# Hybrid Hyena/GLA layer with a PEER expert mixer on one Trainium2 core: two of five token tiles by gathered rows instead of one, their values summed on TensorE in 32-column groups

## What is computed

```python
def peer_ffn(h, wq, sub_keys, u_tab, v_tab):
    q = (x @ wq).reshape(T, PEER_HEADS, 2, PEER_DQ // 2)      # 8 heads, two halves of 128
    s = jnp.einsum('thpd,hpkd->thpk', q, sub_keys)            # 128 sub-keys each
    s_top, i_top = lax.top_k(s, 16)
    cand_s = s_top[:, :, 0, :, None] + s_top[:, :, 1, None, :]
    cand_i = i_top[:, :, 0, :, None] * 128 + i_top[:, :, 1, None, :]
    best, pos = lax.top_k(cand_s, 16)
    idx, gate = take_along_axis(cand_i, pos), softmax(best)
    a = gelu(einsum('td,tkd->tk', x, u_tab[idx]))             # 128 experts per token
    y = einsum('tk,tkd->td', gate * a, v_tab[idx])
```

## Time and profile before

| | us |
|---|---|
| median of 3 runs | 2315.78 (2309.94 to 2328.16) |
| profiled execution | 2312.32 |
| span of its trace | 2310.5 |
| PE busy in the span | 2174.2 (94%) |
| DVE / POOL / ACT busy | 1439.6 / 797.5 / 624.0 |
| data moved by DMA | 475.54 MB |

### The profile page before, as it was taken

The page is one execution under the profiler, slowest core; times in us unless marked ns, Lnnn a source line. Parts: engine busy times, 40 slices in busy tenths (PEclk is TensorE's granted clock), DMA queues, the critical chain, the costliest instruction groups (busy, mean ns, idle before and its releaser), DMA issues.

```text
span 2310.5 us, 30679 instructions
## 1 busy us (share of the span) xinstructions
PE 2174.2 (94%) x9868; PEld 1663.6 (72%) x9868; DVE 1439.6 (62%) x3055; ACT 624.0 (27%) x930; POOL 797.5 (35%) x713
## 2 busy tenths in 40 slices
PE   6999989598998899999989999999999999999998
PEld 2554444445997787787868777787888888888886
DVE  4222322623889999788868877324766666666665
ACT  2111022233212222333323323223322323223232
POOL 0000001002323555799979999101221222212210
PEclk8999998798999999999999999999999999999999
DMA  9122134105102444599988999755988888888883
GB/s 339 41 73 73 42 109 153 64 35 191 62 13 96 155 141 136 165 292 296 301 268 288 302 284 301 233 202 184 359 287 289 292 285 294 287 287 294 285 292 145
DMA packets 293477, 475.54 MB, mean 206 GB/s; under 512 B 148871, under 2 KB 150055, under 8 KB 292872
## 3 DMA queue, kind: packets, MB, share of 16 engines
q1 hardware_dynamic: 256520, 340.20, 44.6%
q0 software_dynamic: 36864, 134.23, 16.4%
HBM read 401.76 MB, written 72.61 MB: 205 GB/s over the span
## 4 chain that ended last, share of the span: by engine, by line
PE 64%; POOL 9%; DVE 5%; issue 2%; DMA 2%; ACT 1%; SPq 1%; DVEq 0%; ACTq 0%; POOLq 0%
PE ps L959 30%; PE ps L900 19%; POOL eB L1846 6%; PE ps L837 3%; POOL ugat L1815 3%; PE ps L872 2%; PE ps L873 2%; PE ps L940 2%; PE ps L719 1%; SPq L523 1%; DMA ugat<-in_u_rows,idx 1%; DMA uraw<-in_u_t 1%; PE ps L861 1%; PE ps L819 0%; DVE h2T L1293 0%
## 5 line engine op out<-in xcount | busy, mean ns | idle before, releaser
L900 PE MATMUL ps<-h2hi,uhi 128*128 128x512 f32 x1024 | 449.1, 439 | 23.4 <-POOL ulo L1803 8.3
L900 PE MATMUL ps<-h2hi,ulo 128*128 128x512 f32 x1024 | 405.5, 396 | 0.0
L959 PE MATMUL ps<-vhi,whi 128*128 128x512 f32 x1024 | 399.8, 390 | 5.2 <-DVE wlo L1467 5.2
L900 PE MATMUL ps<-h2lo,uhi 128*128 128x512 f32 x1024 | 403.6, 394 | 0.0
L959 PE MATMUL ps<-vlo,whi 128*128 128x512 f32 x1024 | 399.7, 390 | 0.0
L959 PE MATMUL ps<-vhi,wlo 128*128 128x512 f32 x1024 | 399.5, 390 | 0.0
L1823 POOL DMA_INDIRECT vgat<-in_v_tab,idx x128 | 149.8, 1170 | 654.7 <-DVE y L1477 504.8
L1846 POOL TENSOR_SCALAR eB<-iota,jcur 128x128 f32<-128x128 f32 x384 | 315.9, 836 | 15.9 <-DVE jcur L1432 14.0
L1465 DVE TENSOR_TENSOR vlo<-vraw,vhi 128x1024 fp32r<-128x1024 f32 x128 | 156.8, 1225 | 216.3 <-ACT vhi L1739 216.3
L1739 ACT ACTIVATE vhi<-vraw 128x1024 fp32r<-128x1024 f32 x128 | 135.5, 1061 | 464.4 <-PE ps L959 462.0
L940 PEld LDWEIGHTS ps<-eA,eB 128*128 128x128 f32 x1024 | 189.8, 189 | 90.0 <-POOL eB L1846 29.9
(11 more groups left out here) (270 smaller groups left out, 2908.7 us busy)
## 6 DMA issues: line engine op xcount, KB each, us to landing
uraw<-in_u_t SPq DMA_DIRECT2D x128, 512.0 KB
vraw<-in_v_tab SPq DMA_DIRECT2D x128, 512.0 KB
gelu_scratch<-aout SPq DMA_DIRECT2D x128, 256.0 KB
gate_scratch<-gst SPq DMA_DIRECT2D x16, 2048.0 KB
ain<-gelu_scratch SPq DMA_DIRECT2D x128, 256.0 KB, 4.2
gin<-gate_scratch SPq DMA_DIRECT2D x128, 256.0 KB, 4.4
wring<-in_w_ada SPq DMA_DIRECT2D x12, 2048.0 KB, 7.8
wring<-in_w_in SPq DMA_DIRECT2D x6, 2048.0 KB, 8.4
```

Of the source, the lines that this page charges most:

```text
L900: last = pe.matmul(ps[:, b % 4, :], w[:, b % 2, k, :], h[:, k, LP:T], start=(k == 0 and j == 0), stop=(k == KD - 1 and j == 2))
L959: last = pe.matmul(ps[:, y_bank(t) + h, :], w[:, b, (t - 1) * P:t * P], v[:, b, h * 512:(h + 1) * 512], start=(start and j == 0), stop=(st ...
```

## The change

- NSP = 2: tiles 0 and 1 go the gathered way (256 tokens); TD becomes 384, three dense tiles. First products have 384 columns, second products are 18 per block. The query products are cut in 256 and 384 columns instead of 320 and 320.
- BLK_A is 48; stage B has 48 blocks (three tiles of 16); stage C has 32 (96 to 127).
- 256 u gathers and dots: 96 in stage B (2 a block, as before), 96 in stage C (3 a block), 64 in the blocks 0 to 31 of the second pass (2 a block).
- The values of the two tiles are no longer added on DVE. For each token POOL gathers its 128 v rows onto the 128 partitions (index column from `idxT`, the turned index; eight buffers `vgat`). The 128 weights of a token are put in one column of a 128 x 32 matrix of zeros (`wcol`), and PE multiplies it with the gathered rows: four tokens to a step, one in each group of 32 output columns, 2 x 4 products of 512 columns (plain float32). 64 such steps stand behind every second block: from block 111 of stage C to block 45 of the second pass for tile 0, from block 50 to block 112 for tile 1.
- gate_scratch is [half tile, partition, block, 64 tokens]: a store is one run of 16 KB per partition; the gates are loaded for four blocks in one DMA in runs of 1 KB.
- The GELU tile is 192 KB a block. h2hi, h2lo and many buffers are placed elsewhere; POOL starts h2lo only when the last output projection is done; the prompt's and the second tile's h2 rows are turned on PE (four more transposes for two halves), and the second tile's rows wait in `h2turn` for a copy after the last query product.
- The loops over registers become unrolled code in several places.

```diff
-TD = T - P
+CG = 32
+NSP = 2
+LSP = NSP * P
+TD = T - LSP
 NTD = TD // P
-BLK_A = 40
+BLK_A = 48
+VSLOT = 8
+DOTS_T = 3
+DOTS_V = 2
+GELU_0 = BLK_C + -(-(HK - NTD * DOTS_IT) // DOTS_T)
+TURN_0 = GELU_0 + 2
+STEP_0 = range(TURN_0 + 2 - NBLK, TURN_0 + 2 - NBLK + 2 * CG, 2)
+GELU_1 = (NDOT - DOTS_A) // DOTS_V
+TURN_1 = STEP_0[-1] + 3
+STEP_1 = range(TURN_1 + 2, TURN_1 + 2 + 2 * CG, 2)
...
-    g_dram = nc.dram_tensor("gate_scratch", [NBLK, P, TD], F32, kind="Internal").ap()
+    g_dram = nc.dram_tensor("gate_scratch", [NHALF, P, NBLK, THALF], F32, kind="Internal").ap()
...
-                sp_.dma_start(g_dram.rearrange("i p (c t) -> c p i t", t=64)[bass.ds(c, 1)]
-                              .rearrange("o p i t -> (o p) i t")[:, ii], gst[:, half, ii]).then_inc(g_stored[half], 16)
+                sp_.dma_start(g_dram[bass.ds(c, 1)].rearrange("o p i t -> (o p) i t")[:, ii], gst[:, half, ii]
+                              ).then_inc(g_stored[half], 16)
...
+            def load_gates(m):
+                if m >= 2:
+                    sp_.wait_ge(w_ready, R2 * (m - 1))
+                sp_.dma_start(gin[m % 2][:].rearrange("p c i t -> p c (i t)"),
+                              g_dram[:, :, R2 * m:R2 * (m + 1), :].rearrange("c p i t -> p c (i t)")).then_inc(g_landed[m % 2], 16)
...
-                        last = pe.matmul(ps[:, b % 4, :], w[:, b % 2, k, :], h[:, k, LP:T],
+                        last = pe.matmul(ps[:, b % 4, 0:TD], w[:, b % 2, k, :], h[:, k, :],
...
+            def weights_to_slots(t):
+                pe.wait_ge(w0_ready, t + 1)
+                pe.transpose(ps[:, 4, 0:P], dots[:, t, :], ident[:]).then_inc(w_turned, 1)
+
+            def value_step(t, r):
+                if r == 0:
+                    pe.wait_ge(wcol_ready, t + 1)
+                g = (t * CG + r) * NCG
+                for c in range(NCG):
+                    pe.wait_ge(v_gathered[(g + c) % VSLOT], 16 * ((g + c) // VSLOT + 1))
+                for h in range(2):
+                    for c in range(NCG):
+                        last = pe.matmul(ps[c * CG:(c + 1) * CG, 4 + h, :], wcol[t][:, c, r, :],
+                                         vgat[(g + c) % VSLOT][:, h * 512:(h + 1) * 512], start=(r == 0), stop=(r == CG - 1))
+                last.then_inc(v_used, 1)
...
+            for n in range(NBLK - R2):
+                second_ready(n)
+                for t in range(NSP, NT):
+                    last = second_products(n % R2, t, n == 0, False)
+                last.then_inc(s2_used, 1)
+                for t, r in steps_at(n):
+                    value_step(t, r)
...
+            dve.wait_ge(h2row_ready, 1)
+            for t in range(NSP):
+                best_experts(t)
+                seq(dve.scalar_tensor_tensor(selw[:, t, 0], selw[:, t, 0], float(NKEYS), selw[:, t, 1], ALU.mult, ALU.add))
+                dve.tensor_copy(idxs[:, t], selw[:, t, 0]).then_inc(idx_ready, 1)
...
+            for n in range(BLK_C, NBLK):
+                if n + 1 < NBLK:
+                    split_u(n + 1, n + 1)
+                for g in tail_dots(n):
+                    dot(g)
...
+            for n in range(NBLK):
+                if n + 1 < NBLK:
+                    weight(n + 1)
+                low_parts(n)
+                for g in value_dots(n):
+                    dot(g)
...
-                    add_value(it, b, first)
...
+            def gather_v(g):
+                if g >= VSLOT:
+                    pool.wait_ge(v_used, (g - VSLOT) // NCG + 1)
+                t, r, c = g // P, (g % P) // NCG, g % NCG
+                tok = c * CG + r
+                pool.indirect_dma_start(out=vgat[g % VSLOT][:], out_offset=None, in_=v_tab,
+                                        in_offset=bass.IndirectOffsetOnAxis(ap=idxT[:, t, tok:tok + 1], axis=0)
+                                        ).then_inc(v_gathered[g % VSLOT], 16)
...
+            for n in range(BLK_C, NBLK):
+                for g in tail_dots(n):
+                    gather_u(g + GSLOT)
+                if n == BLK_C + 2:
+                    for b in range(2):
+                        pool.wait_ge(g_stored[b], 32 * NTD)
+                    pool.memset(wcol[0][:], 0.0).then_inc(wcol_zero, 1)
+                if n == TURN_0 - 1:
+                    for g in range(VSLOT):
+                        gather_v(g)
+                for t, r in steps_at(n - 1 - NBLK):
+                    for c in range(NCG):
+                        gather_v((t * CG + r) * NCG + c + VSLOT)
+            for n in range(NBLK):
+                for g in value_dots(n):
+                    gather_u(g + GSLOT)
+                if n == 1:
+                    pool.wait_ge(h_full, NBLK)
+                    pool.memset(wcol[1][:], 0.0).then_inc(wcol_zero, 1)
+                for t, r in steps_at(n - 1):
+                    for c in range(NCG):
+                        gather_v((t * CG + r) * NCG + c + VSLOT)
```

More of the change, by code:

```diff
@@ L85 @@
 KD_1 = 2
-CG = 32
 KV_ORDER = [(0, "f"), (0, "b"), (1, "f"), (4, "b"), (2, "f"), (3, "b"), (3, "f"), (2, "b")]
@@ L427, in bass_hybrid_layer @@
         a_landed = [sem(f"a_landed{b}") for b in range(4)]
-        g_landed = [sem(f"g_landed{b}") for b in range(4)]
+        g_landed = [sem(f"g_landed{b}") for b in range(2)]
         vhi_ready = sem("vhi_ready")
@@ L848, in _ @@
                 ada_cols(i)
-            for h in range(2):
-                transposes(f"hr{h}", [h2T[:, 4 * h + j, 0:P] for j in range(4)])
+            for t in range(NSP):
+                for h in range(2):
+                    transposes(f"hr{t}{h}", [h2T[:, 4 * h + j, rows(t)] for j in range(4)])
             pe.wait_ge(ld_keys, 16)
@@ L918, in slots_to_rows @@
                 for j in range(3):
-                    last = pe.transpose(ps[:, 6 + d % 2, j * P:(j + 1) * P], selw[:, 1 + d, j, :], ident[:])
+                    last = pe.transpose(ps[:, 6 + d % 2, j * P:(j + 1) * P], selw[:, NSP + d, j, :], ident[:])
                 last.then_inc(cl_full, 1)
+                if d == NTD - 1:
+                    for t in range(NSP):
+                        last = pe.transpose(ps[:, 5, rows(t)], selw[:, t, 0, :], ident[:])
+                    last.then_inc(idx_turned, 1)
             loop(pe, BLK_A // 4 - 1, step_a)
@@ L1381, in _ @@
                     best_keys(t, h)
-            for t in range(1, NT):
+            for t in range(NSP, NT):
                 best_experts(t)
@@ L1480, in step_2 @@
-            def step_2(it, first, last):
-                for b in range(TOPK):
-                    n = it * TOPK + b
-                    if not (last and b == TOPK - 1):
-                        weight(n + 1, (b + 1) % R2, it * 64 + 16 * ((b + 1) // R2 + 1))
-                    low_parts(n, b % R2)
-                    add_value(it, b, first)
-            slot_weights(NTD - 1)
-            weight(0, 0, 16)
-            step_2(0, True, False)
-            with dve.Fori(1, IT_2 - 1) as it:
-                step_2(it, False, False)
@@ L1700, in stage, with slot_gelu @@
                                    ACT.Copy).then_inc(gate_staged, 1)
-            def slot_gelu(r, first):
-                act.wait_ge(dot_done, DOTS_IT * (r + 1))
-                if not first:
-                    act.wait_ge(w0_ready, r)
-                act.activation(acur[:], dots[:], ACT.Gelu_apprx_tanh).then_inc(dots_gelu, 1)
+            def slot_gelu(t):
+                act.wait_ge(dot_done, HK * (t + 1))
+                act.activation(dots[:, t], dots[:, t], ACT.Gelu_apprx_tanh).then_inc(dots_gelu, 1)
             for b in range(4):
@@ L1718, in _, with step_b @@
                 pair(n, n % 4, False, False)
-            def step_b(it, first, second):
+            def step_b(it, first):
                 for b in range(NB_B):
@@ L1831, in _ @@
             pool.wait_ge(idx_ready, 1)
-            for k in range(GSLOT):
-                gather_u(k)
+            for g in range(GSLOT):
+                gather_u(g)
             with pool.Fori(POOL_FROM // 4, BLK_A // 4) as it:
```

428 lines of the change are left out of this document (223 added, 205 removed).

## The result

The changed kernel takes 2361.86 us (median of 4 runs, 2357.52 to 2376.02); the kernel before took 2314.65 us beside it (4 runs, 2309.94 to 2328.16). The ratio is 1.0207, with a 95% interval of 1.0156 to 1.0258. The forecast was 2288 us: the time lies inside the range, but the direction is wrong, 2% slower where 1.2% faster was forecast. The interval shows a slower kernel; whether by more or less than 2% it leaves open.

A forecast was written before the change was run, and what follows sets the result against it. It took PE to bound the second pass, DVE's search stage A, and POOL beside PE stage B. Terms: 707 + 239 + 358 + 247 + 720 + 9 + 3 = 2283 us of span, 2288 as median; range 2230 to 2375.

The forecast's parts named there:

- Front: Ahead of stage A: added turns, moves and a later h2lo cost some 2 us (bounds 0 and 5), 707 us.
- A: Stage A: DVE's top-16 search still ends it, so PE's gain is nearly lost; 239 us.
- So I take 7.34: Stage B: POOL's round is 7.34 us a block once 256-byte gate stores go; 48 x 7.34 + 6 = 358 us.
- POOL stays at 8.26: Stage B rival: slow rounds come from DVE and gathers, not gate stores; 44 us more, 2332; chance 0.07.
- At 390: Behind stage B: transfers run at 390 GB/s, giving stage C 247 us and the second pass 720 us.
- slow rival: Block 108 to second-pass block 112: engines give 354 GB/s, u gathers queue behind v gathers; 2359 us; chance 0.25.
- their 81: Stage C, blocks 96 to 107: 12 x 6.0 us plus 9 for first loads of the second pass, 81 us.
- Blocks 0 to 32: Second pass, first 33 blocks: transfers bound them, 100.1 MB at 390 GB/s, 257 us.
- Blocks 33 to 112: Second pass: PE is full, 80 x 4.09 + 39 x 1.85 = 399 us, three lost, 402 us.
- the rival of 6.89: Value steps: the four column groups run one after the other, 6.89 us a step; 2482 us; chance 0.03.
- the 1.85 us of `ada`: Value steps on PE: 1.85 us each, read from eight like products, with the tiling-mode change taken as inside.
- the three that were to be lost: Second pass, blocks 33 to 112: 3 us lost beyond PE's 399, making 402.

The follow-up runs named there:

- experiment 6: Kernel before and changed kernel each run once more, unchanged: 2321.03 us and 2370.51 us (one run each).
- e4: Kernel before with the partition-major gate scratch alone: 2312.43 us (10 runs), ratio to before 0.9993.
- e7: Changed kernel with stage B's dots replaced by one-element copies (96 of 256 dots missing): 2295.7 us (one run).
- e8: Kernel before with both the partition-major gate scratch and four of eight eB rows on DVE: 2288.99 us (4 runs), ratio to before 0.9850.
- e6: Kernel before with four instead of two of eight eB rows on DVE: 2345.84 us (4 runs), ratio to before 1.0092.
- e5: e3 with two of the four value gathers of a step issued one block later: 2300.55 us (4 runs), ratio to before 0.9922.
- e1: Changed kernel with six u buffers instead of four and six v buffers instead of eight: 2384.0 us, ratio to before 1.0264.
- e12: e5 with the u gathers behind stage B cut to half of each row: 2243.17 us (one run).
- e3: Changed kernel with four instead of two of eight eB rows on DVE: 2313.91 us (10 runs), ratio to before 0.9983.
- e9: e5 with the u gathers behind stage B cut to 64 of 128 partitions: 2331.62 us (one run).

## Why the prediction was wrong

- **Front, +13.** As much can come with an execution alone (experiment 6). The means of the five profiles with the old front and the nine with the new are 714 and 721 us; how much of these 7 us is the change's, for which the prediction had 2, stays open.
- **A, +2.** Right for its stated reason: DVE's search ended it. The 2 us are the reading's: the prediction began B before at 942, where its first product stands at 947, and from 241.3 us A went to 241.7. The search itself was held up more. DVE's L1445 took 4158 ns on average, 3327 in the same operation before: each record takes 2.29 or some 4.37 us, every slow one with POOL's ulo beside it for more than 2 us, and 9 of 10 are slow instead of 4.
- **B, +29: a step that failed.** It said that POOL's slow rounds come with the gate stores, "So I take 7.34". e4 gave 514 us with the stores mended, as before, and rows no faster (858 ns on average, 836 before). What sets the round is DVE: a row takes 1.40 us beside a long DVE operation and 0.62 without (e7). The rival "POOL stays at 8.26" had the right mechanism and 0.07 of the chances; 8.06 was measured. So the shorter round never came: on average it was 8.03 us before (514 / 64) and 8.06 after. The gate layout isn't worthless, but its worth appears only once the rows have been moved (e8 against e6: 59 us in B).
- **C, +38: the larger step that failed.** "At 390" took one rate for all that stands behind B. In C the transfers gave 355 GB/s, because they were not asked for in time: the u gathers queue behind batches of four value gathers. The slow rival named this order, but priced it as a lower rate of the engines. Reordering gives 18 us in C (e5), two more u buffers 27 (e1). The rate is 26 of the 38 us: C moved 101 MB (285 us at 355 GB/s), and at 390 they take 259. Of these 26, 23 are in blocks 108 to 127 (66 MB at 344 GB/s). The other 12 are bytes: 95.9 MB were counted, and forgotten were the last two gate stores, 4 MB, which are issued at the start of C. They are most of what blocks 96 to 107 took over their 81.
- **Blocks 0 to 32, -14.** Right mechanism (bytes, e12), rate too low: 415 instead of 390. The Trainium skill (DMA: Bandwidth & Descriptors, Specifications) puts the limit of HBM at about 358 GB/s per core. It is no ceiling here: 415 held for 243 us. So the total near the slow rival's 2359 is luck: that rival wanted 354 GB/s up to block 112 and nothing lost in B, and the time came from B and C.
- **Blocks 33 to 112, +7.** PE full, as forecast. Column groups in parallel, as forecast; the rival of 6.89 falls. A small step of the prediction fails here: it read the price of changing between the two kinds of products as inside the 1.85 us of `ada`. It stands outside, and a step cost 2.10 us: 39 x 0.25 = 10 us, less the three that were to be lost and weren't.

B and C together are 67 of the 74 us, enough to turn 1.2% faster into 2% slower. In words: PE lost 151 us of busy time, but the whole kernel moves 101 MB more (576.66 against 475.54), and of the four stretches behind A only the last is PE's. With stage B cured and the gathers in the other order (e5) the change is worth 0.8%; the same cure of stage B in the kernel before (e8) is worth 1.5% without it. So in the forms measured here the second gathered tile gains nothing over a kernel of four dense tiles whose stage B runs well: behind the front both take the same, 1574 us in e5 and 1576 in e8, and the medians are 2300.55 and 2288.99.

## What to carry to other kernels

Before work moves from a full engine to the transfers, sum the bytes for each stage and ask when each gather can be issued, behind which others on its queue: a rate that the engines can give isn't reached by an order that asks late. Take the duration of a small GpSimd operation by what VectorE does at its start (here 0.62 or 1.40 us), not as a mean. An edit that shows nothing alone may be half of a pair: try it again once its neighbour is mended.

## What the runs showed of the hardware

- A 128 x 128 compare on POOL takes 0.62 us, and 1.40 when it starts beside a 1024-element operation of DVE (185 and 103 of 288 rows, changed kernel). The other way, a DVE operation of 2048 elements took 2.29 or some 4.37 us; each slow one had a 1024-element operation of POOL beside it, but not each that had one was slow.
- The DMA engines gave 415 GB/s for 243 us with u and v gathers, loads and PE at work together (changed kernel; 248 us in e3).
- A share near 1 is not a rate: 285 to 303 GB/s at 0.97 to 1.03 with gathers onto 64 partitions (e9).
- Eight fp32 products of 512 columns into four column groups cost 2.10 us between fp32r products, 0.25 more than the same eight in `ada`; the 0.25 lies at the changes between the two kinds.
- The same front took 705 and 718 us in two executions of the same kernel, with a granted clock of 0.97 and 0.67 of 2.4 GHz from 360 to 380 us.
